# Constant products in TensorE's waits, and five reorderings, in a two-block transformer kernel

## The chip, the core and the metric

One core of a Trainium2 chip runs the whole program in one launch. The metric is the device time in microseconds. Before the change three runs took 2544.28, 2546.43 and 2540.88 us (median 2544.28). One further execution was recorded by the profiler: 2541.53 us, of which 2539.5 us lie between its first and its last instruction (the span). All rows below come from that execution.

## What is computed

Everything is float32. The first block works on 512 tokens of width 1024, the second on 528 (16 meta tokens come in front).

```
# first block
proj = rmsnorm(x) @ w_in                      # q, k, v of two kinds of heads
sb   = stick_breaking_attention(8 heads)      # w = exp(log_beta + reverse cumulative sum of log_1m)
d    = differential_attention(4 heads)        # (softmax(q1 k1) - lam * softmax(q2 k2)) @ v, rmsnorm per head
x    = x + concat(sb, d) @ w_o
x    = x + (silu(h2 @ w_gate) * (h2 @ w_up)) @ w_down          # h2 = rmsnorm(x)
# second block
u    = rmsnorm(concat(meta, x))
conf = conf_a * sigmoid(conf_g); conf = silu(layer_norm(conv31(conf))) @ w_conf_out
xs, B, C = silu(conv7(u @ w_xbc)); dt = softplus(u @ w_dt + bias)
y    = ssd_scan(forward) + ssd_scan(backward) + D * xs         # 4 groups of 8 heads, chunks of 128 tokens
y    = rmsnorm(y * silu(z)) @ w_ssm_out
h    = h + (g1 * conf + g2 * y) @ w_out
h    = h + expert_choice_ffn(rmsnorm(h))      # 16 experts, 66 tokens each, 384 MB of weights
out  = rmsnorm(h)[16:]
```

## The kernel before

Every engine has its own program (a block each for TensorE, ScalarE, VectorE, GpSimd and the DMA queue SyncE), and runs it strictly in order; semaphores join them. A tile of results is a tag, such as `("c", h)` or `("xb", g, t)`, that owns one or two of the eight PSUM banks: `open_(tag, banks)` makes TensorE wait until the last owner was read, `fill` says that the tag is written, `got(engine, tag)` waits for that, and `free` and `freed` say that it is read. So TensorE's order is written out by hand, and a wait placed early holds up all that stands behind it.

Dense products split each operand into a high part (rounded by ScalarE) and a low part (the rest, by VectorE), and TensorE adds high by high, high by low and low by high. `ffn_high`/`ffn_low`, `tail_split_high`/`tail_split_low` split weights; `x_high`/`x_low`, `y_high`/`y_low` and `merged_high`/`merged_low` split what they are multiplied with.

The stages up to the scan's end, in order, with the lines of the steps:

- Stick-breaking attention: `scores` (L600), the cumulative sums `("c", h)` (L689), rotation (L701), outputs (L716). For a head h > 0 the way to its sums is: VectorE subtracts the sums of head h-1 (L1907) and makes the terms of h (L1864), GpSimd masks both (L2457, four instructions each), then TensorE. GpSimd also makes `cos_part` and the sums `SUMMED` of masked blocks.
- Differential attention: 16 steps (4 heads by 4 query blocks). In step n TensorE makes `diff_scores(n)` (L674), turns the map of step n-3 (L729) and multiplies the turned map of step n-4 with V (L739); VectorE and ScalarE make the softmax between (L1929, L1931, L1360) and ScalarE copies the turned map out of PSUM (L1381). Then `subln_sum` (L750) and `wo` (L760).
- Feed-forward (L785, L786, L789); its first product takes the eight k-tiles of its operand as VectorE finishes `x_low` for each.
- `norm_total("n3")` (L585), the dt product (L830, 16 float32 products of 264 columns against `u_ready`).
- The projections (L843, 5.85 us each; `xb` to the scan's convolution, `ca` and `cg` to the gated 31-tap convolution, then `zt` and gates). Among the first six stand the small products for the scan: dt turned (L887), `F` (L895), `TOT` (L900), `FR` (L905). ScalarE takes each projection out; VectorE runs the 7-tap convolution (L2147) and, wherever a call of `some_taps` stands, taps of the 31-tap one (L2093, L2096).
- The scan, 4 groups of 5 chunks: for a chunk, VectorE makes the masked decays (L2176, L2180), may do taps, multiplies the turned output of the chunk before with its gate (`gate_y`, L2078, which frees bank 5), then adds up the outputs (L2190 to L2210). TensorE needs bank 5 for the chunk's own product `yd` (L996). In the last group ScalarE also squares finished rows (L1617), GpSimd adds the squares (L2532) and scales the inputs (L2512, `XD` among them), both in one queue.
- The dense tail (L1031, L1036): scan output, convolution output, then `("out", m)`, whose operand is `merged`; after `("out", 1)` comes `route(0)` (L1082), which reads the residual H. H is loaded back from memory when `("co", 7)` is filled; the first expert loads wait for `merged` 8.
- Routing and the 16 experts (L1163).

## Time and profile before

| | |
|---|---|
| three runs, median | 2544.28 us |
| profiled execution | 2541.53 us |
| its span | 2539.5 us |
| TensorE busy | 2426.1 us, 96% of the span |
| VectorE, ScalarE, GpSimd busy | 1609.6, 821.5, 412.8 us |
| chain that ended last | TensorE 72%, DMA 17%, VectorE 7% |
| mean granted clock of TensorE | 0.983 |

The chain of waits and work that ended last runs through TensorE for almost three quarters of the span, and through the experts' loads for most of the rest. A busy share counts an instruction as busy however slowly it runs, so idle time and the granted clock are both to be read beside it: at 1.00 the clock is 2.4 GHz, at 0.50 it is 1.2 GHz. Idle time of an engine other than the one that sets the end costs nothing by itself.

### The profile page before, as it was taken

Reading aid. Unit: us, or ns where it says so; the run is one execution under the profiler, and the core shown is the slowest. Engines: PE = TensorE matmul, PEld = TensorE weight load, DVE = VectorE, ACT = ScalarE, POOL = GpSimd, SP = SyncE. Lnnn points to the kernel's source line nnn. Section 1 sums busy time; section 2 is a strip of 40 time slices with the busy share of each in tenths; the row PEclk is TensorE's granted clock in tenths of the full one; section 3 lists DMA queues with packets and bytes.
Section 4 is the critical chain, followed back from the end, with each engine's and each line's share of the span. In section 5 each row is a group of like instructions: output and inputs, shape, how many; then the busy total and the mean of one; then the engine's idle time right before and its main releaser. Section 6 shows DMA issues by size and latency. Waiting matters only on the chain.

```text
span 2539.5 us, 41032 instructions
## 1 busy us (share of the span) xinstructions
PE 2426.1 (96%) x17615; PEld 1532.6 (60%) x17615; DVE 1609.6 (63%) x1749; ACT 821.5 (32%) x1361; POOL 412.8 (16%) x423
## 2 busy tenths in 40 slices
PE   8998899999989999999999979999999999999996
PEld 6764468888879898989989963333322323232322
DVE  4346556665538899998585542766666666666663
ACT  3256644444434646464555330100000000000001
POOL 0034011111101312123531300110010101111100
PEclk9999999999989999999999989999999999999998
DMA  5200278877745555556624558999999999999995
GB/s 199 88 34 26 79 243 289 287 283 264 280 164 187 156 195 156 196 156 206 183 105 160 208 203 313 411 410 412 412 412 413 411 412 413 413 413 410 411 413 229
DMA packets 129718, 676.31 MB, mean 266 GB/s; under 512 B 19301, under 2 KB 52069, under 8 KB 100229
## 3 DMA queue, kind: packets, MB, share of 16 engines
q1 hardware_dynamic: 56624, 554.81, 55.0%
q0 software_dynamic: 25632, 88.49, 10.4%
q10 hardware_dynamic: 47284, 30.42, 4.3%
q8 instruction: 140, 2.29, 0.4%
q14 instruction: 38, 0.30, 0.0%
HBM read 618.55 MB, written 55.12 MB: 265 GB/s over the span
## 4 chain that ended last, share of the span: by engine, by line
PE 72%; DMA 17%; DVE 7%; ACT 2%; issue 2%; POOL 1%; ACTq 1%; SPq 0%; POOLq 0%; DVEq 0%
PE PS L1163 23%; PE PS L843 13%; DMA expert_ring_high<-w_experts 12%; PE PS L789 5%; PE PS L785 5%; PE PS L786 5%; PE PS L1031 4%; DMA expert_ring_low<-w_experts 2%; PE PS L1036 2%; PE PS L689 1%; PE PS L640 1%; PE PS L636 1%; PE PS L637 1%; DVE SQ L2147 1%; PE PS L760 1%
## 5 line engine op out<-in xcount | busy, mean ns | idle before, releaser
L1163 PE MATMUL PS<-expert_ring_high,U 128*32 128x512 f32 x4240 | 472.4, 596 | 18.9 <-DMA expert_ring_high<-w_experts 18.2
L1163 PE MATMUL PS<-expert_ring_low,U 128*32 128x512 f32 x4016 | 446.9, 593 | 10.0 <-DMA expert_ring_low<-w_experts 8.1
L843 PE MATMUL PS<-XH,RINGF 128*128 128x264 f32 x2304 | 392.4, 289 | 1.2 <-ACT arena L1516 1.2
L1163 PEld LDWEIGHTS PS<-expert_ring_high,U 128*32 128x32 f32 x4240 | 136.2, 110 | 330.2 <-issue 302.6
L843 PEld LDWEIGHTS PS<-XH,RINGF 128*128 128x128 f32 x2304 | 323.8, 189 | 9.6 <-issue 7.3
L1163 PEld LDWEIGHTS PS<-expert_ring_low,U 128*32 128x32 f32 x4016 | 128.8, 110 | 308.6 <-issue 289.4
L2363 DVE SCALAR_TENSOR_TENSOR arena<-expert_ring_low,U,arena 128x2048 f32<-128x2048 f32 x134 | 305.7, 2346 | 0.0
L843 PE MATMUL PS<-UH,RINGF 128*128 128x264 f32 x1152 | 233.3, 285 | 0.0
L2096 DVE SCALAR_TENSOR_TENSOR H<-arena,par,H 128x528 f32<-128x528 f32 x240 | 192.4, 845 | 1.3
L843 PEld LDWEIGHTS PS<-UH,RINGF 128*128 128x128 f32 x1152 | 178.9, 189 | 0.0
L2363 DVE SCALAR_TENSOR_TENSOR arena<-expert_ring_high,U,arena 128x2048 f32<-128x2048 f32 x76 | 174.0, 2347 | 0.5
L2605 POOL DMA_INDIRECT residual_rows<-H,scatter_rows x16 | 29.6, 1851 | 849.6 <-DVE H L2394 849.6
L1784 ACT ACTIVATE H<-PS 128x512 f32<-128x512 f32 x32 | 19.1, 597 | 408.8 <-PE PS L1163 408.8
L785 PE MATMUL PS<-UX,WF 128*128 128x512 f32 x352 | 138.6, 394 | 2.1 <-DVE UX L1830 2.1
L786 PE MATMUL PS<-UX,WF 128*128 128x512 f32 x352 | 137.1, 389 | 0.0
L1972 DVE TENSOR_TENSOR RINGF<-ring,WF 128x1024 fp32r<-128x1024 f32 (+1 forms) x76 | 82.4, 1084 | 60.7 <-ACT WF L1420 60.6
L1420 ACT ACTIVATE WF<-ring 128x1024 fp32r<-128x1024 f32 (+1 forms) x76 | 72.0, 947 | 141.9 <-PE PS L789 129.2
L2512 POOL TENSOR_TENSOR arena<-arena,ring 128x512 f32<-128x512 f32 (+1 forms) x32 | 64.5, 2019 | 311.2 <-ACT arena L1597 257.2
L2147 DVE SCALAR_TENSOR_TENSOR SQ<-arena,par,SQ 128x528 f32<-128x528 f32 x144 | 109.7, 766 | 6.2 <-ACT SQ L1504 3.6
L1794 ACT ACTIVATE SQ<-PS 2x512 f32<-2x512 f32 x32 | 18.9, 591 | 271.7 <-PE PS L1163 271.3
L2372 DVE TENSOR_TENSOR H<-H,PS 128x512 f32<-128x512 f32 x32 | 22.0, 688 | 126.4 <-ACT H L1784 88.4
L1962 DVE TENSOR_TENSOR PREL<-arena,PS 128x1024 fp32r<-128x1024 f32 x62 | 75.5, 1219 | 40.8 <-ACT PS L1401 40.0
(358 smaller groups left out, 3866.5 us busy)
## 6 DMA issues: line engine op xcount, KB each, us to landing
expert_ring_low<-w_experts SPq DMA_DIRECT2D x96, 2048.0 KB, 27.1
expert_ring_high<-w_experts SPq DMA_DIRECT2D x96, 2048.0 KB, 30.4
arena<-w_proj POOLq DMA_DIRECT2D x72, 512.0 KB, 5.4
projection_low_parts<-PREL POOLq DMA_DIRECT2D x72, 512.0 KB, 4.3
ring<-w_proj SPq DMA_DIRECT2D x72, 512.0 KB, 3.6
RINGF<-projection_low_parts SPq DMA_DIRECT2D x72, 512.0 KB, 4.7
ring<-w_gu SPq DMA_DIRECT2D x11, 2048.0 KB, 10.3
ring<-ssd_sums ACTq DMA_DIRECT2D x32, 512.0 KB, 9.4
```

What stands on the lines that cost most here:

```text
L785: nc.tensor.matmul(PS[:, bank, :], hi[:, k, :], src[:, 0, k0 + k, :], start=(start and k == 0), stop=False)
L786: nc.tensor.matmul(PS[:, bank, :], hi[:, k, :], src[:, 1, k0 + k, :], start=False, stop=False)
L789: last = nc.tensor.matmul(PS[:, bank, :], lo[:, k, :], src[:, 0, k0 + k, :], start=False, stop=(stop and k == n - 1))
L843: last = nc.tensor.matmul(PS[:, banks[i], 0:HT], w[:, k, :], x[:, k, lo:hi], start=start, stop=stop)
L1031: nc.tensor.matmul(PS[:, banks[i], 0:HT], wh[:, k, :], x(k)[:, lo:hi], start=(first and k == 0 and x is high), stop=False)
L1163: mm = nc.tensor.matmul(PS[QUAD * t:QUAD * t + QUAD, bank, :], stat(t), move(t), start=start, stop=stop)
L1420: A(split_high(p), raw(p), ACT.Copy).then_inc(S("weights_high"), 1)
L1962: V_.tensor_tensor(PREL[:, q % STAGE, :], pre_raw(q), pre_high_place(q).bitcast(F32), SUB).then_inc(S("pre_low"), 1)
L1972: V_.tensor_tensor(split_low(p), raw(p), split_high(p).bitcast(F32), SUB).then_inc(S("weights_low"), 1)
L2096: ins = V_.scalar_tensor_tensor(acc, CP[:, u % 3, j:j + T2], par[:, w0 + j:w0 + j + 1], acc, MUL, ADD)
L2147: V_.scalar_tensor_tensor(co, xp[:, k:k + T2], par[:, w0 + k:w0 + k + 1], co, MUL, ADD)\
L2363: ins = V_.scalar_tensor_tensor(LACC[:, a, :], w, XG[:, k, a:a + 1], LACC[:, a, :], MUL, ADD)
```

## The change

1. TensorE gets products of constants, whose results are overwritten, in front of waits (`fill_wait`): 3 before the sum for the third norm; 2 for heads 0 and 7; 2 of 256 columns before the first turned map; 4, 1, 1 and 2 of 128 columns in the steps of differential attention; 3 of 256 columns before the first `subln_sum`; 2 before the dt product; 3 before the scan's last turned output. Where the bank was opened behind the wait, it is now opened before.
2. The small products are spread: dt is turned after `conf(0, 0)` instead of `conf(0, 1)`, and FR comes after `conf(1, 0)`. ScalarE and VectorE follow: the first two 7-tap convolutions go ahead of the copies of dt, gating and 16 taps ahead of reading F, gating and 8 taps ahead of the exponentials' results; ScalarE takes `conf_gate(1)` ahead of the exponentials.
3. High and low parts go ahead of weight splits: at the first feed-forward, at the scan's end (the split of the first tail weights goes ahead of the squares there), and at `merged`. The last k-tile of `("out", 0)` is multiplied after the low products of the other seven.
4. `gate_y` goes ahead of the first taps of a chunk.
5. GpSimd makes head 0's `cos_part` after its masked sums.

```diff
+            def fill_wait(bank, n, at=0, width=512):
+                for _ in range(n):
+                    nc.tensor.matmul(PS[:, bank, at:at + width], ones, consts[:, 0:width], start=True, stop=True)
...
                 open_(nm, *banks)
+                if nm == "n3":
+                    fill_wait(6, 3)
                 pe.wait_ge(S("squares_added"), ADDS[nm] + DT - 1)
...
+                    open_(("c", h), 3, 4, 5)
+                    if h in (0, SB_HEADS - 1):
+                        fill_wait(3, 2)
                     pe.wait_ge(S("sp_masked"), 4 * h + 1)
-                    open_(("c", h), 3, 4, 5)
...
+                    open_(("at", m), 4 + m % 2)
+                    if m == 0:
+                        fill_wait(4, 2, width=256)
                     pe.wait_ge(S("diff_map"), m + 1)
-                    open_(("at", m), 4 + m % 2)
...
-                    pe.wait_ge(*freed(("at", m)))
                     if qb == 0:
                         open_(("do", h), 6 + h % 2)
+                    fill_wait(6 + h % 2, (4, 1, 1, 2)[qb], at=qb * P, width=P)
+                    pe.wait_ge(*freed(("at", m)))
...
+                open_(("sl", h), 6 + h % 2)
+                if h == 0:
+                    fill_wait(6, 3, width=256)
                 pe.wait_ge(S("subln_sq"), h + 1)
-                open_(("sl", h), 6 + h % 2)
...
             pe.wait_ge(S("dt_in"), 16)
+            pe.wait_ge(*freed(last_tag[4]))
+            fill_wait(4, 2)
             open_("dt", 6, 7)
...
             conf(0, 0)
-            conf(0, 1)
             pe.wait_ge(S("dt_done"), 2)
...
+            conf(0, 1)
             pe.wait_ge(*freed(("dtT", 0)))
...
             fill(last, "TOT")
+            conf(1, 0)
             open_("FR", 4, 5)
...
             fill(last, "FR")
-            conf(1, 0)
             conf(1, 1)
...
+                if (g, c) == (GROUPS - 1, NC - 1):
+                    pe.wait_ge(*freed(last_tag[0]))
+                    fill_wait(0, 3)
                 pe.wait_ge(*freed(("yd", g, c)))
...
+                ahead = DT - 1 if (kind, m) == ("out", 0) else DT
+                for k in range(ahead):
+                    by_high(k)
+                pe.wait_ge(S("weights_low"), TAIL_LOW + p + 1)
+                for k in range(ahead):
+                    last = by_low(k)
+                for k in range(ahead, DT):
+                    by_high(k)
+                    last = by_low(k)
...
-                if m >= DT - FBUF - 1 and m < DT - 1:
+                if DT - FBUF - 1 <= m < DT - 2:
                     ffn_high(m - (DT - FBUF - 1))
+            ffn_high(FBUF - 1)
...
             conf_gate(0)
+            conv_silu(0, 0)
+            conv_silu(0, 1)
             got(act, "FR")
...
+            conf_gate(1)
             act.wait_ge(S("w2_arg"), 2)
...
-            conf_gate(1)
...
+                    if g == GROUPS - 1 and c == 3:
+                        tail_split_high(0)
                     if g == GROUPS - 1 and c < QB:
                         for k in range(3 * c, 3 * c + 3):
                             squared_output(k)
...
             for m in range(DT):
-                tail_split_high(20 + m)
                 if m >= 1:
                     merged_high(m - 1)
+                tail_split_high(20 + m)
...
-                if DT - FBUF <= m < DT - 1:
-                    ffn_low(m - (DT - FBUF))
-            ffn_low(FBUF - 1)
+                if m == DT - FBUF:
+                    ffn_low(0)
+            for p in range(1, FBUF):
+                ffn_low(p)
...
+            conv(0, 0)
+            conv(0, 1)
             for part, dst in enumerate((DTT, AAT)):
...
+            conf_in(0)
+            some_taps(HALF_TAPS, 1)
             got(dve, "F")
...
+            conf_in(1)
+            some_taps(8, 2)
             dve.wait_ge(S("ssd_exp"), 7)
...
-                    chunk_taps(g, c)
-
                     if c > 0:
                         gate_y(g, c - 1)
+                    chunk_taps(g, c)
...
             for m in range(DT):
-                tail_split_low(20 + m)
+                if m >= 1:
+                    merged_low(m - 1)
+                if m < DT - 1:
+                    tail_split_low(20 + m)
                 got(dve, ("co", m))
...
-                if m >= 1:
-                    merged_low(m - 1)
+            tail_split_low(20 + DT - 1)
             merged_low(DT - 1)
...
             for i in range(SB_HEADS + 1):
-                if i < SB_HEADS:
...
+                if 0 < i < SB_HEADS:
+                    cos_part(i)
...
+                if i == 0:
+                    cos_part(0)
```

## Rows read from the trace of the kernel before

**Rows 1.** Windows: stretch, length, busy us (PE, PEld, DVE, ACT, POOL), clock, DMA share, GB/s

```profile
232.00:284.40 52.40, 38.52 (x194) 24.07 (x193) 35.43 (x82) 35.10 (x103) 2.31 (x6) 0.87 0.09 31
...
714.60:724.40 9.80, 9.80 (x33) 5.45 (x33) 4.88 (x11) 5.03 (x8) 0.00 (x0) 0.74 0.68 281
...
747.90:772.20 24.30, 21.97 (x158) 20.65 (x157) 5.14 (x17) 10.78 (x19) 0.00 (x0) 0.79 0.31 96
772.20:1274.60 502.40, 497.28 (x3790) 460.06 (x3790) 433.01 (x571) 262.91 (x553) 147.47 (x102) 1.00 0.56 179
1274.60:1294.00 19.40, 13.20 (x80) 11.07 (x81) 16.98 (x26) 17.77 (x36) 6.20 (x5) 0.74 0.35 137
...
1522.90:2539.50 1016.60, 968.31 (x8872) 305.91 (x8872) 632.27 (x473) 92.18 (x157) 94.45 (x47) 0.99 0.97 394
```

**Rows 2.** Timeline, attention: start, us, engine, line, operation, shapes, [idle before <- releaser]

```profile
239.31 0.33 PE L729 MATMUL PS<-consts_sb,arena 128*128 128x128 f32 x1 [0.70 <-DVE arena L1943]
...
251.03 0.33 PE L729 MATMUL PS<-consts_sb,arena 128*128 128x128 f32 x1
...
255.12 0.49 PE L739 MATMUL PS<-arena 128*128 128x128 f32 x2 [0.64 <-ACT arena L1381]
...
261.48 0.33 PE L729 MATMUL PS<-consts_sb,arena 128*128 128x128 f32 x1
...
279.85 3.13 PE L739 MATMUL PS<-arena 128*128 128x128 f32 x14
284.38 1.10 PE L750 MATMUL PS<-SQ,consts_sb 128*128 128x512 f32 x2 [1.41 <-ACT SQ L1408]
```

**Rows 3.** TensorE's waits up to 1420 us: who for whom, total, times, longest

```profile
PE PS L689 <- POOL arena L2457: 4.6, 2, 2.3
PE PS L996 <- DVE arena L2078: 4.2, 8, 0.9
```

**Rows 4.** Timeline, sums of heads 0 and 1

```profile
159.87 3.09 PE L689 MATMUL PS<-arena,consts_sb 128*128 128x512 f32 x14
...
169.11 4.76 PE L689 MATMUL PS<-arena,consts_sb 128*128 128x512 f32 x14 [2.28 <-POOL arena L2457]
```

**Rows 5.** Timeline, first feed-forward: a weight split, and TensorE's wait

```profile
344.62 1.22 DVE L1972 TENSOR_TENSOR RINGF<-ring,WF 128x1024 fp32r<-128x1024 f32 x1
...
347.28 0.50 PE L785 MATMUL PS<-UX,WF 128*128 128x512 f32 x1 [1.55 <-DVE UX L1830]
```

**Rows 6.** Timeline, third norm and dt product

```profile
711.11 1.13 PE L585 MATMUL PS<-U,consts_sb 128*128 128x264 f32 x4 [3.03 <-DVE U L1838]
...
714.60 9.81 PE L830 MATMUL PS<-U,arena 128*64 128x264 f32 x32 [2.36 <-DVE U L2026]
```

**Rows 7.** Timeline, small products of the scan, first convolution and turn

```profile
749.78 3.35 PE L895 MATMUL PS<-ring,consts_sb 128*128 128x32 f32 x20 [1.08 <-DVE ring L2041]
...
777.65 3.05 DVE L2147 SCALAR_TENSOR_TENSOR SQ<-arena,par,SQ 128x528 f32<-128x528 f32 x4
...
779.24 0.76 PE L918 MATMUL PS<-consts_sb,SQ 128*128 128x128 f32 x5 [0.96 <-ACT SQ L1586]
```

**Rows 8.** Timeline, scan's end: squares added, outputs summed, first tail product

```profile
1278.63 1.58 POOL L2532 TENSOR_TENSOR SQ<-SQ,arena 128x528 f32<-128x528 f32 x1 [4.99 <-ACT arena L1617]
...
1284.02 0.68 DVE L2194 TENSOR_TENSOR ring<-ring 16x512 f32<-16x512 f32 x1 [2.04 <-POOL ring L2512]
...
1285.55 0.57 PE L927 MATMUL PS<-consts_sb,ring 16*128 16x16 f32 x4 [3.09 <-DVE ring L2210]
...
1293.77 2.10 PE L1036 MATMUL PS<-UH,RINGL 128*128 128x264 f32 x16
```

**Rows 9.** Timeline of the first `out` product, and the reload's DMA issue (KB, us to landing)

```profile
1437.59 0.51 PE L1031 MATMUL PS<-XH,WH 128*128 128x264 f32 x2 [1.51 <-DVE MGL L2124]
...
1443.18 1.22 DVE L2114 TENSOR_TENSOR RINGL<-ring,WH 128x1024 fp32r<-128x1024 f32 x1 [4.84 <-DMA H<-residual]
...
H<-residual POOLq DMA_DIRECT2D x1, 2112.0 KB, 9.7
```

More of the change, by code:

```diff
@@ L1670, in _ @@
                             y_high(k)
-                    if g == GROUPS - 1 and c == 3:
-                        tail_split_high(0)
                         tail_split_high(1)
@@ new lines, in _ @@
+            conv(0, 0)
+            conv(0, 1)
+            for part, dst in enumerate((DTT, AAT)):
+                got(dve, ("dtT", part))
+                link(V_.tensor_copy(dst[:, 0:4, :], PS[:, 4 + part, 0:256].rearrange("p (c n) -> p c n", c=4)))
+                free(V_.tensor_copy(dst[0:META, 4, :], PS[0:META, 4 + part, 256:320]), ("dtT", part))
+            dve.wait_ge(*freed(("dtT", 1)))
+            for n, cs in ((P, slice(0, 4)), (META, slice(4, 5))):
+                V_.tensor_scalar(LD[0:n, cs, :], DTT[0:n, cs, :], 1e-30, None, ALU.max).then_inc(S("dt_done"), 1)
```

141 lines of the change are left out of this document (68 added, 73 removed).

## The prediction, made before the change was run

> **What bounds the kernel now.** I read the windows by stage first, then TensorE's waits and the timeline around each, then the DMA view. After 1523 us the experts' stage takes 1016.6 us with the DMA engines 97% busy [rows 1]; nothing there is changed and its first eight loads are long in by then, so what is saved before it is saved in full. Before it TensorE is the bound almost everywhere: in 772 to 1275 it is busy 497.3 of 502.4 us [rows 1]. What is left to win is small: idle time, and stretches where its granted clock is at the lower level (1.2 instead of 2.4 GHz). A mean of 0.87 over the 52.4 us of differential attention, 0.74 over the 9.8 us of the dt product, 0.79 over the 24.3 us around the small scan products and 0.74 over the 19.4 us at the scan's end [rows 1] make (1 - clock) x 2 x length = 13.6, 5.1, 10.2 and 10.1 us at the lower level. Each follows idle time or small products. A stretch at half clock costs half its length only where TensorE itself sets the end.
>
> **Price of a filler.** A product of 128 columns takes 0.226 us at full clock (the last ones of differential attention, 14 passes, 7 products, took 3.13 at half clock); one of 512 takes 1.10 as recorded, with its pipeline end, and 0.86 in a row, 256 columns 0.43 [rows 2]. A filler costs nothing while the wait behind it is longer; beyond that it costs its own time, twice that at the lower clock.
>
> **Stick-breaking heads.** For head 7 two fillers (1.7 us) lie in one of the two waits for GpSimd's mask, 4.6 us together [rows 3]: 0. For head 0 there is no wait: its L689 starts at 159.87 straight behind the scores [rows 4], as its mask was made long before. The two fillers delay it by 1.7 us, and head 1 depends on it (VectorE's subtraction, two masks on GpSimd, then L689 at 169.11 after 2.28 us idle [rows 4]); from there TensorE runs without a gap to 223 us. I count +1.7. Moving `cos_part(0)` behind head 0's sums gains nothing: those sums are done 2 us before they are read, and VectorE is busy until it needs the product. The clock drop at 170 us (L689 4.76 instead of 3.09 us [rows 4]) follows the idle time, which stays as it is. Bounds: 0 (the drop falls away by luck of position) to +3.4.
>
> **Differential attention.** 32 products of 128 columns, 4, 1, 1, 2 in a head's four steps, 7.2 us in all. The waits they sit in: 0.64 us in the first step of head 1, against 0.90 [rows 2]; elsewhere 0.2 to 1.2 us against 0.23 or 0.45. The overrun is about 0.3 us in all; the chain passes VectorE, ScalarE and TensorE in turn, so I count it. The two wider ones before the first transpose take 0.85 in a wait of 0.70 [rows 2]. Gain: with the clock low the head's period was 11.72 us (239.31 to 251.03), at full clock 10.45 (to 261.48) [rows 2]: 1.27. The second low stretch holds L739's 14 passes in 3.13 us where 1.6 would do, and some more before them [rows 2]: 1.7. The three fillers at the first `subln_sum` (1.28) fit in 1.41 us [rows 2]. I take -2.7; bounds -3.6 (all of it) and +1.5 (clock unchanged, fillers at half clock).
>
> **First feed-forward.** Before its last two k-steps TensorE waits 1.55 and 0.5 us for VectorE's low parts; the weight split `ffn_low(1)`, 1.22 us, stands ahead of them on VectorE [rows 5]. It now goes behind, as `ffn_high(2)` does on ScalarE; that split is wanted only after 16 more matmuls (3.7 us). -1.2; bounds -1.5 and -0.5.
>
> **Third norm and dt.** Three fillers (2.6 us) in 3.03 us idle, two (1.7) in 2.36 [rows 6]: no cost. The dt product took 9.81 us, 5.1 of it at half clock [rows 1, 6], but at full clock it is 16 products of 264 columns, 0.44 each: 7.0. VectorE feeds a step in 0.69, TensorE eats one in 0.88, so TensorE sets it. -2.7; bounds 0 and -2.8.
>
> **Small products spread, gating ahead of taps.** TensorE idled 1.08 us for the copies of the turned dt [rows 7]. They now lie under `conf(0, 1)` (5.85 us), although VectorE does two convolutions first (12 taps of 0.77 [rows 7] from 731.7: done at 742.3, when the transposes are). The wait for the first `turn`, 0.96 [rows 7], goes, as that convolution is done early. The low stretch of 10.2 us [rows 1] lay wholly on busy TensorE: up to 5.1. With projections between them the F and TOT products still stand together (5.9 us at half clock, about 3 at full), so I leave one drop in some executions: -4.6. ScalarE and VectorE take new work ahead: 16 taps before F is read (12 us), then w2, exponentials with two table loads, 8 taps. By their durations VectorE has F read at 764, ScalarE is free at 771.4, when `xb(0, 2)` is filled at 771.5; it is close, so its price is a bound. Sum -6.6; bounds -7.6 and -1.0. The wait of 1.25 us for `freed(ca 1)` stays.
>
> **Gating in the chunk loop.** TensorE waited 8 times, 4.2 us in all, for the gating multiply L2078 (it frees bank 5) [rows 3]; six times in groups 0 to 2 it stood behind one or two taps, 3.3 us. Now it comes first. In odd chunks VectorE then idles for the turned y and does its taps later (+0.4 us), covered by 3 us of slack before the next group's `turn`. In group 3 the last two have no tap ahead. -3.1; bounds -4.0 and +1.
>
> **Scan end.** Here a step is traded. `tail_split_high(0)` (1.0 us of ScalarE) now precedes the squares, and GpSimd's three additions wait for those (the first at 1278.63) [rows 8]; behind them stands the `XD` for which VectorE waited 2.04 us [rows 8]. So y, `turn_y` and `y_low(0)` come 1.0 us later, to 1286.4. The eight `y_low` at 0.7, the gating and the split of 1.2 end at 1293.5; L1036 began at 1293.77 [rows 8]. The fillers (2.6 us in 3.09) and the full clock after them make TensorE faster than VectorE feeds it, nothing more. -0.2; bounds -2 and +1.5.
>
> **Last dense product.** The wait of 1.51 us for the last low part, and 0.1 after it, vanish [rows 9]: `ahead` = 7 puts 14 low products before it. But what is late next is the residual's reload: VectorE stood 4.84 us for it, until 1443.18 [rows 9], then must split (1.22), add (0.70), and ScalarE square (0.65) before `route(0)`: 1445.8, where TensorE now arrives at 1445.3. The experts' first loads also wait for `merged`, which comes 2.4 us sooner; they run against the reload, which took 9.7 us to land [rows 9]. Losing half the engines for that time costs it about 0.8: 1446.6, against 1446.9 before. -0.3; bounds -1.6 and +1. The Trainium skill ("DMA: Bandwidth & Descriptors", Issuing engines are not separate DMA queues) says that transfers issued from different engines run on the same sixteen DMA engines and interleave; by that the -1.6 is not to be had, and without sharing the sum would be 0.8 lower.
>
> **The sum**: +1.7 -2.7 -1.2 -2.7 -6.6 -3.1 -0.2 -0.3 = -15.1, from the profiled 2541.5 (span 2539.5): 2526.4. The three runs before (2540.9 to 2546.4, median 2544.3) lie up to 5 above the profiled one; as clock drops differ from one execution to the next I add half the distance to the median, 1.4: **2528**. The Trainium skill ("TensorE: Matmul & The Clock Gate", What's actually happening) says the gate's timing is independent of the kernel's start. If so, the drop at 170 us is absent in some executions; that would move one of them by 1.7, not the sum.
>
> **Rivals.** (a) *The clock is not held*: the constants and the spread products leave the lower stretches in attention and in the scan's preparation. For it: drops came amid busy small products, not only in idle time. Then attention costs +1, the preparation gives 2.0, the rest as above: -6.8, 2536. (b) *ScalarE or VectorE becomes the bound in the scan's preparation*: `xb(0, 2)` is taken 3 to 5 us late, banks 0 and 1 are late for `xb(0, 4)`. Against it: one projection (5.85 us) of slack. -11.1, 2532. (c) *Slower*: the fillers of attention stand on the chain and run at the lower clock throughout: 32 x 0.45 = 14.5 us, with the heads' four at 1.7 each 6.9 and the real products at half clock 5, less 3 of cover: +23.4 against 14.1 gained elsewhere, +9.3, 2552. It decides once the clock stays low for most of the 52 us; the row of 0.87 speaks against it. (d) *The change does not reach the end*: what is gained is waited away at the residual's reload or the experts' start. The 97% after 1523 hold from there on only, so just the last 2 us can go this way: inside the range.
>
> **Chances.** Forecast 0.64 (2521 to 2533), (a) 0.17, (b) 0.10, (c) 0.04, 0.05 left for a cost not seen that eats most of it (2540 to 2548). A measurement tells about 0.2% from no change, 5 us: faster means below 2539.2. Of (a) a quarter lies above that: faster 0.86, same 0.09, slower 0.05. Range 2519 to 2538.
>
> **What would show it.** Right: no low clock between 232 and 284 and at the dt product (L830 in 7 us), L900 near 1.3 instead of 2.5 us, L996 without waits, L843 without the stop at L895, L1082 now waiting for L1746 behind the reload. Wrong: L689 of head 1 no later than before relative to its scores; L2194's wait at the scan's end unchanged; idle time before the projections of `xb(0, 2)` to `xb(0, 4)` over 1.3 us; a drop in the attention stretch.

## The result, and the profile after

The changed kernel takes 2527.6 us (median of four runs, 2526.6 to 2531.4), the kernel before 2544.1 (four runs, 2540.9 to 2546.4): a ratio of 0.9938, 95% interval 0.9922 to 0.9954. 2528 was predicted, with a range of 2519 to 2538. The profiled execution took 2528.0 us with a span of 2526.0 (before: 2541.5 and 2539.5).

The windows of the changed kernel over the same work as [rows 1] (columns: stretch, length, busy us of PE, PEld, DVE, ACT, POOL, granted clock, DMA share, GB/s); the first is attention, then the dt product, the small scan products, the chunk loop, the scan's end, the experts:

```profile
233.30:283.00 49.70, 43.20 (x269) 29.53 (x267) 35.44 (x82) 34.93 (x103) 2.34 (x6) 1.00 0.09 33
711.71:718.90 7.19, 7.19 (x32) 4.27 (x32) 4.88 (x11) 5.04 (x9) 0.00 (x0) 1.00 0.93 383
742.50:761.40 18.90, 17.65 (x156) 16.89 (x154) 14.49 (x23) 9.06 (x13) 0.00 (x0) 1.00 0.37 121
761.40:1259.20 497.80, 496.41 (x3790) 460.72 (x3790) 407.98 (x547) 267.19 (x561) 144.40 (x102) 1.00 0.56 181
1259.20:1277.00 17.80, 14.40 (x84) 9.38 (x84) 15.39 (x25) 16.70 (x33) 4.91 (x5) 1.00 0.30 112
1509.40:2526.00 1016.60, 968.14 (x8872) 305.56 (x8868) 632.28 (x473) 92.21 (x157) 94.46 (x47) 0.99 0.97 394
```

The clock column is 1.00 where it was 0.87, 0.74, 0.79 and 0.74. Below, "a low stretch" is a stretch in which TensorE's granted clock is at the lower of its two levels. The experts take the same 1016.6 us as before, so what was gained ahead of them arrives at the end. TensorE's waits up to 1420 us, beside [rows 3] (L1015 is the old L996, L698 the old L689, L740 the old L729, L859 a projection, which waits for `freed(ca 1)`):

```profile
PE PS L698 <- POOL arena L2503: 2.6, 2, 2.2
PE PS L1015 <- DVE arena L2166: 2.0, 2, 1.6
PE PS L740 <- DVE arena L1978: 1.8, 2, 1.3
...
PE PS L859 <- ACT arena L1549: 1.2, 1, 1.2
```

L698 still waits 2.2 us at head 1 and only 0.4 at head 7; six of the eight waits for the gating multiply are gone; the 1.25 us for `freed(ca 1)` stayed, as forecast. But one wait of L1015 is now longer (1.6) than any was (0.9).

The timeline shows where this is, and the stretch at the end of the dense products that answers [rows 9] (columns: start, us, engine, line, operation, shapes, [idle before <- releaser]; ACTq is ScalarE's queue issuing a DMA):

```profile
1239.90 1.01 ACTq L1610 DMA_DIRECT2D ring<-ssd_sums  x2
...
1242.55 5.31 ACTq L1563 DMA_DIRECT2D gate_sums<-arena  x1
...
1256.55 1.23 DVE L2221 TENSOR_TENSOR ring<-ring 128x1024 f32<-128x1024 f32 x1 [2.67 <-ACT ring L1621]
...
1259.78 1.97 PE L1015 MATMUL PS<-arena 128*128 128x64 f32 x16 [1.57 <-DVE arena L2166]
...
1416.48 0.57 POOL L2644 DMA_DIRECT2D H<-residual  x1 [16.92 <-PE PS L1058]
...
1418.16 1.36 SPq L2738 DMA_DIRECT2D expert_ring_low<-w_experts  x3
...
1428.18 1.23 DVE L2171 TENSOR_TENSOR RINGL<-ring,WH 128x1024 fp32r<-128x1024 f32 x1 [8.29 <-DMA H<-residual]
...
1430.84 0.65 PE L1114 MATMUL PS<-H,par 128*32 128x264 f32 x2 [2.96 <-ACT SQ L1781]
```

and the DMA view gives the reload (KB, us from issue to landing):

```profile
H<-residual POOLq DMA_DIRECT2D x1, 2112.0 KB, 11.7
```

ScalarE's queue spends 5.3 us issuing one store; behind it stand the squares and exponentials, VectorE's addition of the two decays (L2221; it stood 0.9 us for ScalarE before and 2.7 now) and at last TensorE. And TensorE now stands 2.96 us for H, where it had stood 1.5 us for the last low part: its first routing product has 0.65 us for what takes 0.42 at full clock.

Stage by stage, in us between the same instructions of both timelines (the second begins head 0 about 0.4 earlier, counted from the span's start); the last column is from the executions of the experiments below that have the edit in question (in brackets how many):

| from to | before | after | forecast | measured | others with it |
|---|---|---|---|---|---|
| heads, the fillers of head 0 counted | 66.2 | 67.9 | +1.7 | +1.7 | 67.6 to 67.9 (4); without them 64.7 to 67.7 (8) |
| head 7 to the first `subln_sum` | 58.3 | 55.6 | -2.7 | -2.8 | 55.6 (8), 56.7 (1) |
| feed-forward to second norm | 8.5 | 7.15 | -1.2 | -1.4 | 7.1 to 10.5 (8) |
| second norm to the dt product's end | 373.1 | 370.5 | -2.7 | -2.6 | 370.5 to 371.4 (8) |
| small products to the first chunk | 122.15 | 114.56 | -6.6 | -7.6 | 114.6 (4), 116.1 (5), 117.5 (1) |
| chunk loop, groups 0 to 2 | 383.5 | 380.2 | -3.1 | -3.4 | 379.6 to 381.2 (10) |
| group 3 up to chunk 4 | 51.4 | 52.5 | in the line above | +1.1 | 51.3 to 53.1 |
| chunk 4 to the first low products | 12.36 | 10.87 | -0.2 | -1.5 | 10.9 (8), 11.2 (1) |
| from there to `route(0)` | 153.1 | 153.8 | -0.3 | +0.7 | 152.8 to 154.0 (3); with the loads held back 150.7 to 151.1 (5) |
| routing products, lists, gather | 74.5 | 76.9 | 0 | +2.4 | 74.2 to 76.9 |

### The profile page after: what moved, and what is told of

It reads as the page before. It is cut to its first block, busy times and chain, and to the rows that moved or that the text cites. A ratio compares the mean times of both kernels' runs of the same rounds, so it can differ in the third digit from the quotient of the medians.

```text
span 2526.0 us, 41221 instructions
## 1 busy us (share of the span) xinstructions
PE 2432.1 (96%) x17713; PEld 1536.4 (61%) x17713; DVE 1605.4 (64%) x1749; ACT 823.0 (33%) x1362; POOL 410.0 (16%) x423
## 3 DMA queue, kind: packets, MB, share of 16 engines
q0 software_dynamic: 25632, 88.49, 10.5%
## 4 chain that ended last, share of the span: by engine, by line
PE 76%; DMA 17%; DVE 3%; issue 1%; ACT 1%; POOL 1%; ACTq 0%; SPq 0%; POOLq 0%; DVEq 0%
PE PS L1195 24%; PE PS L859 16%; DMA expert_ring_high<-w_experts 12%; PE PS L803 5%; PE PS L799 5%; PE PS L800 5%; PE PS L1052 5%; PE PS L1058 2%; DMA expert_ring_low<-w_experts 2%; DMA projection_low_parts<-PREL 1%; PE PS L698 1%; PE PS L647 1%; PE PS L643 1%; PE PS L644 1%; PE PS L1015 1%
## 5 line engine op out<-in xcount | busy, mean ns | idle before, releaser
L859 PE MATMUL PS<-XH,RINGF 128*128 128x264 f32 x2304 | 392.2, 289 | 1.2 <-ACT arena L1549 1.2
L859 PEld LDWEIGHTS PS<-XH,RINGF 128*128 128x128 f32 x2304 | 323.2, 189 | 9.8 <-issue 7.3
L859 PE MATMUL PS<-UH,RINGF 128*128 128x264 f32 x1152 | 232.9, 284 | 0.0
L2089 DVE SCALAR_TENSOR_TENSOR H<-arena,par,H 128x528 f32<-128x528 f32 x240 | 186.4, 820 | 2.0
L859 PEld LDWEIGHTS PS<-UH,RINGF 128*128 128x128 f32 x1152 | 178.4, 188 | 0.0
## 6 DMA issues: line engine op xcount, KB each, us to landing
ring<-w_gu SPq DMA_DIRECT2D x11, 2048.0 KB, 10.5
```

The source lines that it names most:

```text
L859: last = nc.tensor.matmul(PS[:, banks[i], 0:HT], w[:, k, :], x[:, k, lo:hi], start=start, stop=stop)
L2089: ins = V_.scalar_tensor_tensor(acc, CP[:, u % 3, j:j + T2], par[:, w0 + j:w0 + j + 1], acc, MUL, ADD)
```

## The experiments

**Does the clock hang on the fillers?** The changed kernel with every filler left out, and the kernel before with the fillers alone. Both edits in short:

```diff
-                for _ in range(n):
+                for _ in range(0):
                     nc.tensor.matmul(PS[:, bank, at:at + width], ones, ...)
```

> The changed kernel with all constant products left out (the order of everything else stays). If the fillers are what keeps the clock in differential attention, two low stretches return there (granted clock about 0.87 over the 52 us) and attention is 2.7 us longer; with head 0's 1.7 us saved, the first feed-forward begins about 1.0 us later than in the changed kernel. At the dt product a low stretch returns and costs 2 to 2.7 us. At the small products, where no filler stands, nothing changes: no low clock between 740 and 775 relative to the stage. At the scan's end a low stretch returns, and costs TensorE 3 to 5 us of which up to 1.5 reach the end, as VectorE's low parts set the pace there. Sum about +5 us. Rival: the low stretches do not hang on the fillers (chance of position); then this kernel is 1.5 us faster than the changed one.

> The kernel before with the constant products alone, no change of order. My theory: attention -2.7 us against the kernel before (no low clock between 232 and 284), heads +1.7 (the two of head 0), third norm and dt -2.7 (the dt product in 7 us instead of 9.8); the small scan products keep their low stretch (10.2 us before), as none is put there, and the gating waits stay; at the scan's end up to -1.5. Sum -4 to -5 us up to the routing. Rival: the fillers alone do nothing for the clock (the stretches stand where they stood): +3 us. The changed kernel without them was 5.8 us slower than the changed kernel up to the scan in one execution, which speaks for the theory.

Measured: 2531.0 and 2547.9 us, against one run of the kernel before on each chip (2547.4 and 2543.7). These are single runs, so what follows goes by stages. Microseconds at the lower clock by stretch, from the windows, as (1 - clock) x 2 x length:

| execution | attention | first feed-forward | dt product | small products | scan's end |
|---|---|---|---|---|---|
| before | 13.6 | 0 | 6.8 | 10.2 | 10.2 |
| before, fillers alone | 0 | 6.8 | 0 | 10.2 | 13.6 |
| before, gating ahead alone | 13.6 | 0 | 6.8 | 10.2 | 6.8 |
| before, spread alone | 13.6 | 3.4 | 6.8 | 3.4 | 10.2 |
| changed, no filler | 13.6 | 0 | 10.2 | 0 | 6.8 |
| changed | 0 | 0 | 0 | 0 | 0 |
| eight others with the fillers of attention and dt | 0 (7), 3.4 (1) | 0 (6), 3.4 (2) | 0 (8) | 0 (3), 3.4 (4), 6.8 (1) | 0 (5), 3.4 (2), 6.8 (1) |

So fillers hold the clock in attention and at the dt product: ten executions with them, one low stretch; four without, 13.6 and 6.8 to 10.2 each time. The rival, that the low stretches stand where they do by chance, fell. Left out of the changed kernel, the fillers were missed by more than I had expected: head 7 to the first `subln_sum` took 60.3 us instead of 55.6 (one more low stretch, at 226 us, among them), the second norm to the dt product's end 3.9 us more, and the heads 3.1 less. At the scan's end they were not missed: 10.88 us from chunk 4 to the first low products, as with them. The small products keep their low stretch without the spread, fillers or not, and lose most of it with the spread, fillers or not. In the rest the fillers alone did worse than I had expected: 4.2 us slower than the kernel before, where I had said 4 to 5 faster up to the routing. The timeline of the kernel with the fillers alone, in the first feed-forward and at the scan's end:

```profile
347.07 0.50 PE L799 MATMUL PS<-UX,WF 128*128 128x512 f32 x1 [2.39 <-DVE UX L1849]
...
1284.40 5.49 PE L583 MATMUL PS<-consts_sb 128*128 128x512 f32 x6
1289.82 0.42 PE L946 MATMUL PS<-consts_sb,ring 16*128 16x16 f32 x4
1290.17 0.51 PE L1050 MATMUL PS<-UH,WH 128*128 128x264 f32 x2
```

The three fillers at the scan's end (six passes) met a low clock and took 5.49 us; VectorE's last sum for y was done at 1285.3, and `turn_y` (L946) began at 1289.82 behind them, so that chunk 4 to `turn_y` took 7.05 us instead of 4.14. In the changed kernel the same six passes took 2.84 us, in a wait of about 3.1. The low products behind came later still (16.6 us after chunk 4 instead of 12.4). A filler that fits only at full clock is a bet on the clock it is to hold. The rest came in the first feed-forward (11.6 us for 8.5: a wait for VectorE and a low stretch behind it) and in group 3 (53.0 for 51.4).

**Head 0.**

```diff
-                    if h in (0, SB_HEADS - 1):
+                    if h == SB_HEADS - 1:
                         fill_wait(3, 2)
```

> The changed kernel without the two fillers of head 0 (head 7 keeps its own). My theory: they stand in no wait and delay the mask chain of head 1 by their 1.7 us; without them head 1's L698 begins 1.7 us earlier than in the changed kernel, the low-clock stretch at 171 us stays (it follows the 2.2 us of idle time, which stay), and all later marks up to the experts are 1.7 us earlier. Rival: the fillers are what keeps a second low stretch away; then L698 of head 0 or the products after it run at half clock and the mark at head 2 is 0 to 2 us later than in the changed kernel.

2531.8 us (one run; the kernel before took 2547.4 on that chip). Head 1's sums began 1.5 us earlier (0.57 us by which that execution began head 0 later taken off), but ran longer at the low clock, and the gain was gone by head 2:

```profile
160.05 3.09 PE L698 MATMUL PS<-arena,consts_sb 128*128 128x512 f32 x14
...
169.38 5.88 PE L698 MATMUL PS<-arena,consts_sb 128*128 128x512 f32 x14 [2.38 <-POOL arena L2503]
```

5.88 us against 4.74 in the changed kernel. One execution settles nothing here. Over all that there are, head 0 to head 7 took 64.7, 64.8, 66.1, 66.2, 66.4, 66.4, 67.4, 67.4 and 67.7 without the fillers (mean 66.3) and 67.6 to 67.9 in five with them: they cost 1.5 us on average. From head 0 to head 1 the cost is the same each time, 10.85 us with them and 9.2 to 9.3 without. The drop behind that took 3.4 us in all five with the fillers; in the nine without it was absent twice, 3.4 us four times and 6.8 three times. What that run lost besides was a low stretch in attention and 6.8 us of low clock at the small products, both absent in others of the same edits; its reload took 11.9 us.

**The reload of H.** The changed kernel with one wait more on SyncE's queue:

```diff
             sp.wait_ge(S("merged"), DT)
+            sp.wait_ge(S("h_moved"), 32)
             for i in range(ERING):
```

> The changed kernel in which SyncE issues the experts' first loads only when the reload of H has landed. My theory: the loads, issued 1.7 us behind the reload, take DMA engines from it; without them the reload lands after 6 to 8 us instead of 11.7, VectorE's first split and addition then wait for TensorE's product 0 instead of for H, the idle time before route(0) falls from 2.96 to about 1.5 us and all marks from route(0) to the first gather are 1.4 us earlier. The stage after 1523 starts with its loads in, so that is also what the end gains. Rival: the reload takes its 10 to 12 us alone (it is bound by its own descriptors), so nothing moves by more than 0.3 us; or the later loads are missed by the first expert, which then waits up to 8 us longer.

And the changed kernel with its last dense product put back (the low parts and products in the order of before):

> The changed kernel with the last dense product put back as it was (products of all eight k-steps by the high weights first; the weight split ahead of the low part of the merged input). In the changed kernel the experts' loads follow the reload of H by 1.7 us instead of 3.5, the reload took 11.7 us instead of 9.7, and route(0) came 0.7 us later relative to the start of the out products' stage than before. My theory: undone, merged comes about 2 us later, the loads with it, the reload lands after 9.5 to 10 us, and route(0) is 0.7 to 1.5 us EARLIER relative to the scan's end than in the changed kernel, though TensorE's wait of 1.5 us for the last low part is back. Rival: the reload's time has nothing to do with the loads' start (it varies from one execution to the next: 10.7 to 11.9 us in three more executions); then route(0) stays where it is, since TensorE waits for H in either order, or comes up to 0.5 us later.

With the loads held back (one run, 2525.1 us) the way from the first low products to `route(0)` took 150.8 instead of 153.8 us, twice what I had expected: VectorE's addition was done before TensorE came, so the whole wait went. The reload landed after 8.3 us, not after 6 to 8 as I had expected. The low stretch at 1431 us went with it, worth about 1.4 by my estimate (half of its 3.4 us is 1.7; from `route(0)` to the gather it took 74.8 us instead of 76.9). The experts took 1016.5 us from their first product to the end, 1016.7 in the changed kernel. The reload in the DMA view with the loads held:

```profile
H<-residual POOLq DMA_DIRECT2D x1, 2112.0 KB, 8.3
```

In the kernel put back (one run, 2533.9 us; 2543.7 for the kernel before on that chip), the reload in the DMA view and TensorE's wait in the timeline:

```profile
H<-residual POOLq DMA_DIRECT2D x1, 2112.0 KB, 9.6
```

```profile
1425.19 0.51 PE L1050 MATMUL PS<-XH,WH 128*128 128x264 f32 x2 [1.51 <-DVE MGL L2168]
```

Over all executions the reload took 8.2 to 8.9 us with no load beside it (five), 8.5 to 9.7 with the loads 3.5 us behind it (five, the order of before), 10.7 to 11.9 with the loads 1.7 us behind (four, the changed order): so the rival that the reload only varies fell, though the first two ranges overlap. With the changed order `route(0)` follows the landing exactly (153.8 for 11.7, 154.0 for 11.9, 152.8 for 10.7, 153.0 for 10.9). The Trainium skill ("DMA: Bandwidth & Descriptors", Issuing engines are not separate DMA queues) says that transfers of different engines interleave on the same DMA engines; the rows agree, and give the price: 1.8 us earlier loads, about 2 us later reload. But that undoing the order would bring `route(0)` 0.7 to 1.5 us earlier is not shown: put back it took 154.4 us, with the wait of 1.51 us again and a low stretch at 1427 us that costs 1.7; without that it would be 152.7, within 0.4 of three of the four other executions with the order of before (153.1; the fourth, 154.6, has a low stretch over the first low products). The reorder thus gives -0.3 to +0.9 by how the reload lands, and -2.3 once the loads wait.

**Gating and spreading, each alone.**

```diff
-                    chunk_taps(g, c)
-
                     if c > 0:
                         gate_y(g, c - 1)
+                    chunk_taps(g, c)
```

> The kernel before with VectorE's gating multiply ahead of the taps in the chunk loop, and nothing else. My theory: TensorE's waits in groups 0 to 2 fall from 4.2 us to under 1 us, so group 3 begins 3.1 to 3.4 us earlier relative to group 0; in group 3 about 1.0 us of it is lost at chunk 3, where ScalarE's chain of decays sets the time. Sum -2.2 us. Rival: the taps moved behind the multiply are missed by the next group's convolution or the gate of chunk 1, and TensorE waits there instead: within 1 us of nothing.

> The kernel before with the spreading of the small scan products (projections between them, ScalarE's and VectorE's work reordered to match) and nothing else. My theory: 2.0 us of idle time go for certain (the copies of the turned dt and the first turn); the low stretch there, 10.2 us in the kernel before, has been 0, 6.8, 3.4, 0 and 0 us in five executions with the spread, so it costs 0 to 3.4 us instead of 5.1. Sum from the end of the dt product to the first chunk: -3.5 to -7.6 us. Rival: the clock's gain hangs on the fillers ahead of it (in the dt product), since those keep the clock up until the small products begin; then the stretch stays near 10 us here and the sum is -2 to -2.5.

Gating alone: 2539.7 us; groups 0 to 2 took 380.8 instead of 383.5 us (-2.8), and group 3 lost nothing (51.3 for 51.4), against what I had expected. Spread alone: 2538.3 us; to the first chunk 116.1 instead of 122.15 (-6.1, with one low stretch of 3.4), the upper half of what I had expected, so the clock's part does not hang on the fillers. But the chunk loop then took 2.1 us more than before:

```profile
866.45 2.02 PE L996 MATMUL PS<-arena 128*128 128x64 f32 x16 [1.48 <-DVE arena L2132]
```

With the taps still ahead of the multiply TensorE waited 1.5 us in the first group, and a low stretch at 868 us followed. No execution with the multiply first has that wait. As far as this one execution shows, the spread needs the gating ahead; I had summed them as independent, which held only because both were in.

**The store that stands behind 64-byte pieces.**

```diff
-                    if g == GROUPS - 1 and c + 2 < NC:
+                    if g == GROUPS - 1 and c < 2:
                         fr_load(g, c + 2)
                     gates_out((g, c))
...
-                    if g < GROUPS - 1 and c + 2 < NC:
+                    if (g < GROUPS - 1 or c == 2) and c + 2 < NC:
                         fr_load(g, c + 2)
```

> The changed kernel with one load of the last group (the decays' arguments of chunk 4, two transfers with 64-byte pieces) issued by ScalarE behind the two gate stores instead of ahead of them. In the changed kernel the first gate store after that load keeps ScalarE's queue 5.3 us; behind it stand the squares, the exponentials of chunk 3, VectorE's multiply L2221 (idle 2.67 us) and TensorE's L1015 (idle 1.57 us), where the gain of the chunk loop is lost again by 1.0 us. My theory: with the store ahead the queue is free 5 us earlier, L2221 no longer waits for ScalarE, L1015's wait falls under 0.4 us, chunk 3 of group 3 begins 1.0 to 1.5 us earlier; the three additions on GpSimd and the XD product come earlier too, so VectorE's wait of 2.03 us at L2238 goes and the scan's end gains 1 to 2 us more. Sum -2 to -3.5 us. Rival: the 5.3 us are the load's own issue cost, which then simply stands behind the stores and delays the squares as before: 0.

2525.1 us. The same rows in this kernel:

```profile
1240.14 0.33 ACTq L1563 DMA_DIRECT2D gate_sums<-arena  x1
...
1246.35 1.33 ACTq L1610 DMA_DIRECT2D ring<-ssd_sums  x2
...
1255.55 1.34 DVE L2221 TENSOR_TENSOR ring<-ring 128x1024 f32<-128x1024 f32 x1 [0.92 <-ACT ring L1621]
...
1258.89 1.97 PE L1015 MATMUL PS<-arena 128*128 128x64 f32 x16 [0.54 <-DVE arena L2166]
...
1268.19 0.68 DVE L2238 TENSOR_TENSOR ring<-ring 16x512 f32<-16x512 f32 x1 [2.05 <-POOL ring L2563]
```

The store takes 0.33 us, chunk 3 comes 1.0 us earlier after chunk 2, as expected (L1015's wait is 0.54 us, not under 0.4); the second half was wrong: VectorE's wait at L2238 is what it was, and the scan's end gained nothing more. The order of load and store is the same in the kernel before, so all nine executions that have it can be read. Load and store together kept the queue 5.0 to 5.1 us in four of them (the kernel before, gating alone, spread alone, no fillers), and L1015 waited 0.54 to 0.61, as it does with the store ahead; they kept it 5.5, 5.9, 6.3, 6.6 and 6.6 us in the five with fillers, and L1015 waited 1.3, 1.2, 1.6, 1.9 and 1.9. So the loss hangs on the queue's time, and not on the gating ahead, by which I had explained it. Why the queue takes longer in the kernels with fillers no run shows.

That it is the short pieces that hold the store up, the changed kernel's own timeline shows: the same two transfers for chunk 2 (128 columns, 512-byte pieces) end 1.6 us ahead of a store just as those for chunk 4 (16 columns, 64-byte pieces) do, and that store takes 0.34 us:

```profile
1211.14 1.01 ACTq L1610 DMA_DIRECT2D ring<-ssd_sums  x2
...
1213.79 0.34 ACTq L1563 DMA_DIRECT2D gate_sums<-arena  x1
```

**Three and four edits together.** Head 0's fillers out, the loads held, the small load behind the store; then also the first weight split back behind the squares; then that without the fillers at the scan's end; and the three with two of six advance splits moved from the output product's stage to the down product's.

```diff
-                    if g == GROUPS - 1 and c == 3:
-                        tail_split_high(0)
                     if g == GROUPS - 1 and c < QB:
                         for k in range(3 * c, 3 * c + 3):
                             squared_output(k)
                     if g == GROUPS - 1 and c == 3:
+                        tail_split_high(0)
                         for k in range(DT):
                             y_high(k)
```

> The changed kernel with three edits: no fillers at head 0 (as in the run without them), the experts' first loads behind the reload of H, and the last group's 64-byte load behind the gate store. If each is worth what its own run showed, they add, as each has its own stretch: head 0 about -1.3 on average (without the fillers head 0 to head 2 took 18.5 to 21.5 us in five executions, with them and their 1.7 us 21.3 to 21.6), the scan's chunk 3 -1.0, the reload -3.0, the clock drop behind the wait for it -1.4. Sum about -6 us against the changed kernel, 2521 to 2523; ratio to the kernel before 0.991. Rival: the experts' first loads come too late for the first expert, or the edits shift the clock's low stretches into other places: ratio 0.993 to 0.994, as the changed kernel.

> The kernel of the three edits with the first weight split of the last stage on ScalarE put back between the squares of chunk 3 and the high parts of y (the change had moved it ahead of the squares). My prediction counted that move at +1.0 us for GpSimd's three additions, XD and turn_y. If so, put back: GpSimd's first addition 1.0 us earlier relative to chunk 3, VectorE's wait of 2.04 us at L2238 falls to about 1.0, turn_y and the first low products (L1058) come 1.0 us earlier, sum -1.0. Rival: VectorE's chain (y_low one by one behind y_high, which now comes 1.0 us later, then two weight splits) sets L1058, and turn_y earlier gives nothing: 0.

> The kernel of the four edits (no fillers at head 0, first expert loads behind the reload, 64-byte load behind the store, first split behind the squares) without the three fillers at the scan's end as well. In the kernel before with the fillers alone they met a low clock there, took 5.49 instead of 2.84 us, and held turn_y by 3.9 us; in the changed kernel without any filler a low stretch of 6.8 us stood there and the marks behind it (from chunk 4 to turn_y 4.14 us, from there to the first low products 6.73 us) were the same as in the changed kernel with them. Theory: they buy nothing, as GpSimd's XD and VectorE's low parts set that stretch: 4.14 and 6.73 us again, low clock or not; median within 1 us of the four edits' 2523.0 and none of the slow tail. Rival: without them the low stretch lasts into the low and high products behind L1058, where TensorE is the bound, and costs 1.5 to 3.4 us up to the routing: median 2525 to 2526.

> The kernel of the three edits with the last two of six advance splits of projection weights in the output product's stage moved to the down product's stage. Their raw weights come one round trip of 6.0 us after another, so ScalarE stands for the sixth (until 335.6 to 338.2 us) with the high parts of the first feed-forward's input behind it; TensorE then waits in the first feed-forward. From its start to the sum of squares it took 7.1 to 8.2 us in five executions of the changed kernel and its variants, 10.5 in one in which a low clock stretch followed the wait, and 6.9 us would be needed without waits. Theory: 6.5 to 7.0 us each time, 0.4 to 1.3 us gained, and the low stretches at 348 us seen in some executions go; ratio 0.0003 to 0.0008 below the kernel of the three edits. Rival: two more splits in the down product's stage delay VectorE or ScalarE there and the gain is given back by the third norm: 0 or slower by 1 us.

| kernel | median, range of five | ratio, 95% interval |
|---|---|---|
| three edits | 2525.1, 2523.0 to 2526.3 | 0.9927, 0.9914 to 0.9941 |
| and the split behind the squares | 2523.0, 2521.6 to 2524.7 | 0.9922, 0.9908 to 0.9936 |
| and no fillers at the scan's end | 2522.4, 2522.1 to 2522.9 | 0.9915, 0.9901 to 0.9928 |
| three edits, two splits moved | 2528.0, 2525.4 to 2529.1 | 0.9939, 0.9926 to 0.9953 |

The medians are 2.5 us below the changed kernel for three edits and 5.2 for five, where I had said 6 for three, and they come from different chips. In the profiled execution of the three edits (2523.4 for 2528.0) the edits' own stretches gave 9 us together: the heads 3.2 us less, group 3 0.7, the way to `route(0)` 2.8, the routing 2.3. Against that the first feed-forward took 2.2 us more (9.4, with a low stretch) and the experts 1.8. The intervals of the best and of the changed kernel overlap; the best kernel's highest run lies under the changed kernel's lowest, but the two were not timed on the same chip. Putting the split back gave 2.1 us between medians with ranges that overlap, where I had expected 1.0 or nothing. Without the fillers at the scan's end the median stayed within 1 us of 2523.0, as expected.

The split, first the kernel with it ahead of the squares (three edits), then with it behind them:

```profile
1261.52 0.69 DVE L2263 TENSOR_TENSOR arena<-arena,ring 128x512 f32<-128x512 f32 x1
...
1262.50 1.12 POOL L2583 TENSOR_TENSOR SQ<-SQ,arena 128x528 f32<-128x528 f32 x1 [5.89 <-ACT arena L1652]
...
1262.96 0.80 DVE L2221 TENSOR_TENSOR ring<-ring 16x128 f32<-16x128 f32 x1
...
1267.41 0.68 DVE L2238 TENSOR_TENSOR ring<-ring 16x512 f32<-16x512 f32 x1 [2.03 <-POOL ring L2563]
```

```profile
1262.52 0.69 DVE L2262 TENSOR_TENSOR arena<-arena,ring 128x512 f32<-128x512 f32 x1
...
1262.60 1.58 POOL L2582 TENSOR_TENSOR SQ<-SQ,arena 128x528 f32<-128x528 f32 x1 [5.00 <-ACT arena L1652]
...
1263.96 0.36 DVE L2220 TENSOR_TENSOR ring<-ring 16x128 f32<-16x128 f32 x1
...
1267.98 0.68 DVE L2237 TENSOR_TENSOR ring<-ring 16x512 f32<-16x512 f32 x1 [2.04 <-POOL ring L2562]
```

Counted from chunk 3 (1258.12 and 1259.12), GpSimd's first addition starts 0.9 us earlier with the split behind, as expected, but XD only 0.4, and so does all that follows. The addition then starts 0.08 us after VectorE's multiply of two tiles in SBUF (L2263, here L2262) and ends 0.97 after that one's end, 1.58 us for 1.12; in the other order VectorE's small addition (L2221) is the one that takes longer (0.80 for 0.36). So XD and VectorE both slip by 0.4 together, which is why L2238's wait does not move between the two. The Trainium skill ("SBUF — State Buffer", SBUF: two separate sides) says that a GpSimd operation that reads SBUF and a VectorE operation with two inputs in SBUF lock the shared port pair for a whole instruction, whoever is first; the rows of these two pairs agree in who gets longer.

The scan's end without fillers:

```profile
1269.67 0.58 PE L943 MATMUL PS<-consts_sb,ring 16*128 16x16 f32 x4 [3.09 <-DVE ring L2250]
1270.35 0.78 PE L1049 MATMUL PS<-UH,WH 128*128 128x264 f32 x2
```

The low clock is back (0.78 for 0.48), and the stretch to the first low products takes 7.09 us instead of the 6.73 that I had expected again. With the split behind the squares the fillers there gave 0.4 us; with the split ahead of them they gave nothing (10.88 us without any filler); and they cost 2.9 where the clock was low.

The two moved splits: the feed-forward took 5.9 us, less than the 6.5 to 7.0 hoped for, but 1.94 us more passed from the second norm to the dt product's end. TensorE now waited there for ScalarE's weight split, itself behind the moved ones (next row; a second wait took 0.23). That the gain is given back, the rival, was right; but the median is 2.9 above the three edits, and these two stages come out even or better, so it is not explained by them.

```profile
686.12 0.50 PE L799 MATMUL PS<-GX,WF 128*128 128x512 f32 x1 [1.10 <-ACT WF L1452]
```

## Why the prediction was right, and where it was not

- **Heads, +1.7: right.** 1.7 in the profiled pair, 1.5 on average. The drop at 170 us stayed (4.74 us for L698, 4.76 before). A sign of "wrong" that I had named did show: L698 of head 1 starts 4.6 us after its scores, 4.7 before. It was a poor sign, as the fillers delay those scores too.
- **Attention, -2.7: right** (-2.8), by its mechanism: no low stretch, and a period of 10.45 us per head.
- **Feed-forward, -1.2: right for the profiled pair** (-1.4; TensorE's wait fell from 1.55 to 0.17 us), but this term varies by 3 us. ScalarE's splits of advance weights wait for loads that come 6.0 us apart; when they are late, so are the high parts of the input. I had read the split behind it and not the load ahead of it.
- **Norm and dt, -2.7: right** (-2.6); the dt product took 7.3 us instead of 9.8.
- **Small products, -6.6: right in the mean.** 7.6 in the profiled pair with no low stretch; the mean of the eleven executions with the spread is 115.5 us, 6.6 less than before. F and TOT took 3.5 us, not 5.9. The step of one drop left in some executions was right (six of eleven).
- **Gating, -3.1: mechanism right, size off, a term missing.** -3.4 in groups 0 to 2; but in group 3 I had said only that no tap stands ahead, and put its cost at nothing. There ScalarE's chain (store, exponentials) bounds TensorE, and 1.1 us went to it. The queue's time for the store (4.1 us in the trace of before) could have been read. This loss is not the gating's: the kernel with gating alone lost nothing in group 3, and the one with fillers alone, its gating unmoved, lost 1.6. Net -2.3.
- **Scan's end, -0.2: the step of the traded 1.0 us failed, and so did its outcome.** Counted from chunk 3, XD comes 0.1 us later in the profiled pair (7.84 for 7.72) and up to 0.4 in others, not 1.0; and VectorE's wait for it is unchanged (2.03 for 2.04), which I had named as a sign of "wrong". And I had VectorE's chain as the bound of L1036, though [rows 8] show no wait for VectorE ahead of it. Two rows of the kernel before that I had not drawn on say why:

```profile
1287.10 0.78 PE L1031 MATMUL PS<-UH,WH 128*128 128x264 f32 x2 [0.97 <-ACT WH L1629]
...
1291.01 2.36 DVE L2114 TENSOR_TENSOR RINGL<-ring,WH 128x1024 fp32r<-128x1024 f32 x2
```

  The first of the two splits was done at 1292.2, TensorE arrived at 1293.77: its high products had begun only when ScalarE's first split was in, and ran at half clock. VectorE's first split ends 10.8 us after chunk 4 in both kernels; in the changed one TensorE is there in time and waits 0.37 us for it, so VectorE is the bound only now. The earlier split gave this 1.5 by itself: without any filler, at the lower clock, the stretch took the same 10.88 us.
- **Last dense product, -0.3: mechanism right, size off.** Reload as the next bound, loads running against it: both there. But I priced the contention at 0.8 us; it was 2.0, so +0.7. And a TensorE that stands 3 us for H can meet a low clock in the routing products (+1.4), which no term had; it did in three of the four executions with a wait of 2.0 to 3.2 us there, and in none of the ten others. Right so far as it went: the gain could be had only with the loads behind the reload.
- The remaining +1.0 of the lists and gathers is in no term; it was 0 to 1.4 in other executions, changed order or not.

The errors of the terms cancel in part: -2.3 at the small products and the scan's end, +4.2 at the chunk loop with its group 3, the reload and the routing, about -0.4 elsewhere. The profiled execution came out 1.6 us above the sum (2528.0 for 2526.4), the median 1.2 above it, and the allowance of 1.4, made for the spread of the clock, stood in for it; that the forecast of 2528 was met to 0.4 us is partly luck. Rival (a), clock not held, showed once in ten executions in attention, and only for 3.4 us; rival (b) did not show, `xb(0, 2)` waits 1.25 us as before; (c) did not occur, but the scan's end of the fillers-alone kernel is its mechanism at another place: a filler at the lower clock, priced twice; (d), which I had bounded to the last 2 us, took 2.1 (0.7 and 1.4).

What is open: why a low stretch falls at 170 us in twelve of fourteen executions, at 226 in two (one has both, one neither); why the queue's time for load and store grows in the kernels with fillers; and whether the five edits hold their 5 us over the changed kernel on one chip, as the two were not timed on the same one.

## What to carry to other kernels

A constant product in a wait holds the clock, but measure the wait at the lower clock: it must be covered there too, or the filler delays what it was to speed up. Of each queue that feeds the bound engine, read in the trace of before how long it is held by what it issues, transfers included: one store of 0.3 us took 5 us behind small pieces. And before a gain sets loads off earlier, look at what they run beside: a wait on the transfer that is needed first was worth more than the reorder itself.

## What the runs showed of the hardware

- Issuing a 128x528 store on ScalarE's queue took 0.33 us alone, 0.34 us behind two loads in 512-byte pieces that ended 1.6 us before it, and 3.6 to 5.6 us behind two loads in 64-byte pieces (16 columns, 128 partitions, 8 heads each) at the same distance.
- A 2.1 MB reload took 8.2 to 8.9 us with no expert load beside it, 8.5 to 9.7 with 2 MB loads issued 3.5 us behind it, 10.7 to 11.9 with 2 MB loads issued 1.7 us behind it.
- A GpSimd addition of 128x528 took 1.12 us alone and 1.58 when it began 0.08 us after a VectorE multiply with both inputs in SBUF.
- How much the clock differs between executions at one place depends on the place: 13.6 us low in attention in all four kernels without fillers, 10.2 amid the small products in all three without the spread, 0 to 6.8 there in eleven with it, and 0 to 6.8 at head 1 in nine without head 0's fillers.
